# Row norms of a two-layer encoder at the stage handovers: root and reciprocal by token instead of spread over 128 rows

## The reference, cut to what matters

```python
def rms_norm(x, g=None):
    y = x * lax.rsqrt(jnp.mean(jnp.square(x), axis=-1, keepdims=True) + EPS)
    return y if g is None else y * g
def modulated_pre(x, g, mods, j):
    return rms_norm(x, g) * (1.0 + mods[:, 3 * j + 1, None]) + mods[:, 3 * j, None]
def gated_post(x, o, g, mods, j, coef):
    return x + coef * mods[:, 3 * j + 2, None] * rms_norm(o, g)
def layer(x, c, l, mixer):
    h = modulated_pre(x, norm_pre[l, 0], mods, 0)
    x = gated_post(x, swiglu(h, ...), norm_post[l, 0], mods, 0, 0.5)
    h = modulated_pre(x, norm_pre[l, 1], mods, 1)
    o, st = mixer(h, l)
    x = gated_post(x, o, norm_post[l, 1], mods, 1, 1.0)
    h = modulated_pre(x, norm_pre[l, 2], mods, 2)
    x = gated_post(x, swiglu(h, ...), norm_post[l, 2], mods, 2, 0.5)
```

## Time and profile before

| | us |
|---|---|
| median of 3 runs | 2572.78 |
| lowest, highest | 2572.46, 2575.69 |
| the profiled execution | 2575.32 |
| its span, first to last instruction | 2573.5 |

### The profile page before, as it was taken

How to read it: one execution, slowest core, us unless ns; L and a number is a source line. 1 busy time by engine, 2 the same in 40 slices (tenths; PEclk the granted TensorE clock), 3 DMA queues, 4 the chain that set the end, 5 groups by cost and what they waited for, 6 DMA issues and landing times.

```text
span 2573.5 us, 43848 instructions
## 1 busy us (share of the span) xinstructions
PE 2374.8 (92%) x17486; PEld 2231.6 (87%) x17486; DVE 1318.2 (51%) x2006; ACT 812.6 (32%) x1371; POOL 893.4 (35%) x384
## 2 busy tenths in 40 slices
PE   1999999899788899999989999989988898999996
PEld 1999999899456899999989999989964588999996
DVE  7333379784473333337253335986835515333552
ACT  2322322433223433223243223234323334223321
POOL 1333334443000544344444343444420034333342
PEclk9999999999899999999999999999989999999998
DMA  6222268323100122226312224761220011222551
GB/s 222 76 88 84 90 236 280 116 88 112 33 1 6 61 89 83 89 89 248 122 57 82 90 81 155 281 221 66 82 71 33 1 50 59 89 84 87 182 197 57
DMA packets 71507, 272.48 MB, mean 106 GB/s; under 512 B 8640, under 2 KB 10048, under 8 KB 70528
## 3 DMA queue, kind: packets, MB, share of 16 engines
q1 hardware_dynamic: 71424, 271.35, 30.6%
HBM read 267.87 MB, written 3.45 MB: 105 GB/s over the span
## 4 chain that ended last, share of the span: by engine, by line
PE 75%; DVE 12%; issue 6%; ACT 3%; DMA 1%; POOL 1%; DVEq 0%; SPq 0%; POOLq 0%; ACTq 0%
PE ps L534 21%; PE ps L533 21%; PE ps L537 21%; PE ps L543 2%; PE ps L831 2%; PE ps L875 2%; DVE ret_q L1407 1%; PE ps L827 1%; DVE ret_k L1407 1%; DVE wide_v L1297 1%; DVE x L1301 1%; PE ps L566 1%; DVE wide_v L1256 1%; POOL w_lo L446 1%; DVE ps L1290 1%
## 5 line engine op out<-in xcount | busy, mean ns | idle before, releaser
L446 POOL TENSOR_TENSOR w_lo<-raw,w_hi 128x1024 fp32r<-128x1024 f32 (+1 forms) x304 | 790.7, 2601 | 1609.8 <-ACT w_hi L947 1294.1
L533 PE MATMUL ps<-h_hi,w_hi 128*128 128x274 f32 x3296 | 897.0, 290 | 5.3 <-DVE z_tmp L1376 5.3
L534 PE MATMUL ps<-h_lo,w_hi 128*128 128x274 f32 x3296 | 900.7, 290 | 0.0
L537 PE MATMUL ps<-h_hi,w_lo 128*128 128x274 f32 x3296 | 686.7, 289 | 0.0
L533 PEld LDWEIGHTS ps<-h_hi,w_hi 128*128 128x128 f32 x3296 | 624.9, 190 | 6.8 <-issue 6.7
L534 PEld LDWEIGHTS ps<-h_lo,w_hi 128*128 128x128 f32 x3296 | 621.7, 189 | 0.2
L947 ACT CAST w_hi<-raw 128x1024 fp32r<-128x1024 f32 (+1 forms) x236 | 268.7, 1138 | 877.3 <-PE ps L537 689.8
L537 PEld LDWEIGHTS ps<-h_hi,w_lo 128*128 128x128 f32 x3296 | 522.0, 188 | 0.0
L533 PE MATMUL ps<-u_hi,w_hi 128*128 128x272 f32 x1408 | 382.4, 289 | 12.9 <-POOL w_lo L446 12.9
L534 PE MATMUL ps<-u_lo,w_hi 128*128 128x272 f32 x1408 | 380.8, 289 | 0.0
L1256 DVE CUSTOM_DVE_ANT_0 wide_v<-ada_w,ps 128x1024 bf16<-128x1024 f32 x288 | 332.1, 1217 | 46.5 <-DMA ada_w<-in_ada 29.3
(11 more groups left out here) (219 smaller groups left out, 2552.5 us busy)
## 6 DMA issues: line engine op xcount, KB each, us to landing
raw<-in_w_up SPq DMA_DIRECT2D x176, 512.0 KB, 3.3
ada_w<-in_ada SPq DMA_DIRECT2D x160, 512.0 KB, 4.4
raw<-in_w_dn SPq DMA_DIRECT2D x64, 704.0 KB, 4.7
raw<-in_w_mix SPq DMA_DIRECT2D x64, 512.0 KB, 3.3
decay<-in_decay SPq DMA_DIRECT2D x2, 2048.0 KB, 8.3
x<-in_x SPq DMA_DIRECT2D x1, 2176.0 KB, 9.1
rope_tab<-in_rope SPq DMA_DIRECT2D x2, 1088.0 KB, 4.9
out_y<-x SPq DMA_DIRECT2D x1, 2176.0 KB, 7.3
```

Of the source, the lines that this page charges most:

```text
L446: pool.tensor_tensor(w_lo[:, slot, 0:width], raw[:, slot, 0:width], w_hi[:, slot, 0:width].bitcast(F32), ALU.subtract).then_inc(lo_done.se ...
L533: pe.matmul(ps[:, bank + t, 0:half], wh, hi[:, n], start=start, stop=False)
L534: pe.matmul(ps[:, bank + t, 0:half], wh, lo[:, n], start=False, stop=False)
L537: last = pe.matmul(ps[:, bank + t, 0:half], wl, hi[:, n], start=False, stop=stop)
```

## The change

Each norm's sums are turned round. `token_sums` takes the tile of squares as the stationary operand, 128 tokens at a time, and a single column of ones as the moving one: five weight blocks (the last overlaps the fourth: tokens 416 to 543) and five matmuls of one column in place of two of 272. The sums land with tokens on partitions, 128x5, in unused columns of the second bank (`by_token`). ACT roots and DVE inverts those 128x5. Then `spread` brings them back: PE waits for the reciprocal and transposes each of the five columns, broadcast to 128 (32 in the last), so that all 128 partitions hold the 544 factors in the two banks. After a sub-layer DVE multiplies straight from there. Before one, DVE waits for the transposes and copies them to `rinv`; PE's wait on the root becomes a wait on that copy (`rinv_in`). `spread` stands at the end of `out_tiles` and at the end of `first_tiles`. The mixer's inner norms still use `add_squares` and `root_of`.

```diff
+TOK_AT = [0, P, 2 * P, 3 * P, T - P]
+TOK = len(TOK_AT)
+SUM_AT = 2 * NS
...
+        tok_root = sb("tok_root", [P, TOK])
+        tok_inv = sb("tok_inv", [P, TOK])
...
-        out_inv = pair(4)
+        def by_token(bank):
+            return ps[:, bank + 1, SUM_AT:SUM_AT + TOK]
+        def along(bank):
+            return ps[:, bank:bank + 2, :].rearrange("p b n -> p (b n)")[:, 0:T]
...
+            def token_sums(src, bank, start, stop):
+                for b, at in enumerate(TOK_AT):
+                    last = pe.matmul(by_token(bank)[:, b:b + 1], src[:, at:at + P], ones[:, 0:1],
+                                     start=start and b == 0, stop=stop, skip_group_check=True)
+                return last
+            def spread(l, n, bank):
+                pe.wait_ge(inverted.sem, inverted.at(l, n + 1))
+                for b in range(4):
+                    pe.transpose(ps[:, bank, b * P:(b + 1) * P], tok_inv[:, b:b + 1].to_broadcast([P, P]), ident[:, :])
+                pe.transpose(ps[:, bank + 1, 0:NS], tok_inv[P - NS:P, 4:5].to_broadcast([NS, P]),
+                             ident[P - NS:P, P - NS:P]).then_inc(inv_spread.sem, 1)
...
@@ first_tiles, pre_sum, early_sum
                 last.then_inc(w_used.sem, 1)
+                spread(l, 2 * j, 6)
...
-                add_squares(tmp_s[:, m % 2, :], 6, m == N_EARLY, False, ones).then_inc(sums.sem, 1)
+                token_sums(tmp_s[:, m % 2, :], 6, m == N_EARLY, False).then_inc(sums.sem, 1)
...
-                add_squares(squares[:, :], 6, False, True, ones).then_inc(sums.sem, 1)
+                token_sums(squares[:, :], 6, False, True).then_inc(sums.sem, 1)
...
@@ up (in the mixer likewise, rinv_in.at(l, 2))
-                pe.wait_ge(rooted.sem, rooted.at(l, 4 * s + 1))
+                pe.wait_ge(rinv_in.sem, rinv_in.at(l, 2 * s + 1))
...
@@ out_tiles
-                add_squares(squares[:, :], 4, True, False, ones)
+                token_sums(squares[:, :], 4, True, False)
                 pe.wait_ge(out_sq.sem, out_sq.at(l, (j + 1) * KD))
-                add_squares(tmp_s[:, 1, :], 4, False, True, ones).then_inc(sums.sem, 1)
+                token_sums(tmp_s[:, 1, :], 4, False, True).then_inc(sums.sem, 1)
+                spread(l, 2 * j + 1, 4)
...
@@ ACT, in pre_scale (bank 6) and out_tiles (bank 4)
+            def token_root(l, n, bank):
+                nc.scalar.activation(tok_root[:, :], by_token(bank), ACT.Sqrt, bias=eps[:, 0:1], scale=1.0 / D)\
+                    .then_inc(rooted.sem, 1)
...
@@ DVE turn_over, post
-                    v_.reciprocal(out_inv, halves(root[:, :])).then_inc(inverted.sem, 1)
-                    dve.wait_ge(inverted.sem, inverted.at(l, 2 * j + 2))
+                    v_.reciprocal(tok_inv[:, :], tok_root[:, :]).then_inc(inverted.sem, 1)
                     dve.wait_ge(out_ev.sem, out_ev.at(l, (j + 1) * KD))
+                    dve.wait_ge(inv_spread.sem, inv_spread.at(l, 2 * j + 2))
...
-                        v_.tensor_tensor(halves(tmp_v[:, m % 2, :]), halves(o_buf[:, m, :]), out_inv, ALU.mult)\
+                        v_.tensor_tensor(tmp_v[:, m % 2, :], o_buf[:, m, :], along(4), ALU.mult)\
...
@@ DVE turn_over, pre
-                    v_.reciprocal(rinv[:, :], root[:, :]).then_inc(inverted.sem, 1)
+                    v_.reciprocal(tok_inv[:, :], tok_root[:, :]).then_inc(inverted.sem, 1)
+                    dve.wait_ge(inv_spread.sem, inv_spread.at(l, 2 * j + 1))
+                    v_.tensor_copy(rinv[:, :], along(6)).then_inc(rinv_in.sem, 1)
```

More of the change, by code:

```diff
@@ L249, in streaming_trunk @@
         inverted = signal("inverted", 6)
+        inv_spread = signal("inv_spread", 6)
+        rinv_in = signal("rinv_in", 3)
         h_high = signal("h_high", 54)
@@ L663, in mixer @@
                 z_tile(3, 2, 1)
-                pe.wait_ge(rooted.sem, rooted.at(l, 3))
+                pe.wait_ge(rinv_in.sem, rinv_in.at(l, 2))
                 norm_sum(0, 0, 6, True, False)
@@ L985, in pre_scale @@
                 act.wait_ge(sums.sem, sums.at(l, (j + 1) * SUMS - 1))
-                root_of(l, rooted, 2 * j, 6, D)
+                token_root(l, 2 * j, 6)
                 high(l, next_chunk + 3, 1, KD * P)
@@ L1040, in out_tiles @@
                 act.wait_ge(sums.sem, sums.at(l, (j + 1) * SUMS))
-                root_of(l, rooted, 2 * j + 1, 4, D)
+                token_root(l, 2 * j + 1, 4)
             def ffn(l, s):
@@ L1325, in ffn @@
                         n = s * FT + i * 2 + f
-                        dve.wait_ge(inverted.sem, inverted.at(l, 4 * s + 1))
+                        dve.wait_ge(rinv_in.sem, rinv_in.at(l, 2 * s + 1))
                         dve.wait_ge(up_mul.sem, up_mul.at(l, 2 * n - 2))
@@ L1371, in z_scaled @@
                     dve.wait_ge(w_used.sem, w_used.at(l, MIX_C0 + z + 1))
-                    dve.wait_ge(inverted.sem, inverted.at(l, 3))
+                    dve.wait_ge(rinv_in.sem, rinv_in.at(l, 2))
                     if z >= 2:
```

## The result

| | before | after |
|---|---|---|
| median, us | 2572.6 (4 runs) | 2608.1 (4 runs) |
| lowest, highest | 2571.0, 2575.7 | 2607.0, 2610.2 |
| span of the profiled execution | 2573.5 | 2608.4 |

The changed kernel is slower: ratio 1.0128, 95% interval 1.0113 to 1.0142, or 36 us. The forecast was 2614.0 in a range of 2570 to 2631.

A forecast was written before the change was run, and what follows sets the result against it. PE was three quarters of the chain of waits, so time is won where PE idles. The profiled 2575.3 with -8.8 post, +7.5 pre and +43 clock gives 2616.8, for the median 2614; range 2570 to 2631.

The forecast's parts named there:

- The clock: Pre stages: PE falls to 1.2 GHz after two sums; 7.1 us a stage, 43 in six (24 to 60); chance 0.72.
- the doubled sums: Pre stage at half clock: three token sums take double the time, +3.35 us a stage.
- The rest of the spell in the next tile: After a pre stage: the half-clock stretch runs on into the next weight tile, +1.0 us a stage.
- the clock that holds: Rival: PE's clock doesn't fall in the pre stages; -1.3 us, 2571.5, no change; chance 0.16.
- Post: After a sub-layer: shorter chain from sum to first product; 1.2 us in five handovers, 2.75 in the last, 8.8 together.
- The wait for POOL: After a sub-layer: DVE's add to `x` ends 0.59 us after POOL's `w_lo`, so five handovers gain 1.2, not 2.75.
- Pre: Before a sub-layer, clock aside: removed root and reciprocal worth nothing, added weight loads and transposes cost 7.5 us in all.
- The row with the same load: Profile row for token sums: 128-column loads every 0.1115 us, so a sum of ten records takes 1.12 us.
- the row of narrow matmuls at 0.034: Profile row with 64-column weights and 32 moving columns, 0.034 us apart; lower bound of 0.34 us for a token sum.
- Cheap loads: Rival: weight loads of the token sums clearly under 0.09 us and the clock holds; 19.4 us faster, 2553; chance 0.06.
- spread stalls: Rival: PE's `spread` waits because ACT casts the next chunk before the root; some 2580 us; chance 0.03.
- chain not shortened: Rival: after a sub-layer the chain from sum to first product stays as long; takes off the 8.8, 2623; chance 0.03.

The follow-up runs named there:

- 128 columns: Changed kernel with the five pre sums moving 128 equal columns of ones per matmul in place of one: 2578.9 us, ratio 1.0011 to the kernel before.
- pre alone: Changed kernel with by-token norms only before a sub-layer, those after one as in the kernel before: 2616.4 us, ratio 1.0158 to the kernel before.
- runs with 32 columns: Changed kernel with the five pre sums moving 32 equal columns of ones per matmul in place of one: 2581.9 us, ratio 1.0024 to the kernel before.
- 64 and 128 columns: The 64-column version: changed kernel with pre sums moving 64 equal columns of ones per matmul in place of one: 2577.4 us, ratio 1.0008 to the kernel before.
- post alone: Changed kernel with by-token norms only after a sub-layer, those before one as in the kernel before: 2568.7 us, ratio 0.9978 to the kernel before.
- The cast moved ahead: By-token norms only after a sub-layer, with ACT's next-chunk cast and root before its last output copies: 2564.0 us, ratio 0.9955 to the kernel before.

## Why the prediction was right

**The clock, which decided.** It fell in all six pre stages, as forecast, and six stages cost 29.2 us by it in their own length (changed kernel against 128 columns). I had 3.35 + 2.0 + 0.75 = 6.1 a stage, 36.6 in all; measured are 4.2 to 6.3. The mis-sized term is the doubled sums: I let the clock fall after two sums everywhere. In the profile of the changed kernel it did so only before the mixers, the second and fifth sub-layers (stages of 17.2 and 16.7); in the other four it fell after three, so two were doubled and not three, 1.0 us less. That is no rule of these places: in pre alone, with the same pre stages, lengths are 14.0 to 16.7 and the clock fell before or within the third sum in four of six. What sets the place stays open. The second tile's 16 matmuls cost 1.7 more (4.00 against 2.28 with 128 columns; I had 2.0), `spread` 0.4 to 0.5 (0.75). The rest of the spell in the next tile was at most 0.5, not 1.0: after the first stage the third tile's first six matmuls take 1.37 us, with 128 columns 0.87. It was 0.4 to 0.5 in four stages, 0.1 in the fourth and nothing in the second, 1.9 in all where I had 6.
The evidence was weaker than I took it for. I argued from matmuls of 32 columns beside which the clock stayed at 1.2 GHz. The runs with 32 columns show that this width, once the clock is at 2.4 GHz, holds it in five stages of six. What the row showed was a clock that was down already and didn't rise, in a stretch where PE also had gaps; that it would fall under single columns didn't follow from it, and the 0.16 for the clock that holds was low for what was known. That the clock fell in all six stages was therefore partly luck.
The Trainium skill, page "TensorE: Matmul & The Clock Gate", section Part 1: The HAM clock gate, ties the clock to the array's activity. The runs agree in so far as less was computed in the stages that fell (six, one, none and none of six with 1, 32, 64 and 128 columns); the profile's busy columns are not a measure of it, since they are full on both sides.

**Post.** Forecast 8.8, measured 8.6. The chain by its terms, from post alone: the sum ends 0.23 later (forecast 0.24), root 0.27 (0.22), reciprocal 0.19 (0.18), transposes 0.82 (0.8), and from them to the product 0.11 (0.04). The first product starts 3.80 us after the first sum's start, 2.64 earlier than before; I had 2.75. That a 128x5 root and reciprocal could be had from 128x1 and 128x544 by a line was right to 0.05 us. The wait for POOL was right: 0.59 after POOL's end was the assumption, 0.57 and 0.58 were measured, and 1.19 of 1.2 us were gained. The cast moved ahead gives the other 1.45 back in the stage, which only a run could show.

**Pre.** The token sums: ten loads every 0.1118 us, 1.17 by the records, forecast 0.1115; at half clock 0.213. The row with the same load was the right one, and the row of narrow matmuls at 0.034 was not. The growth without the clock came to 1.72 + 5 x 1.09 = 7.2 against the 7.5 of the sum, `spread` 0.69 of the 0.75. Root, reciprocal and copy hid as said: DVE still waits 4.5 us for PE before its copy at 81.1.
The Trainium skill's section LDWEIGHTS on the page just named, columns / 1.2, gives 107 ns for these loads, as an estimate. The 0.112 measured agrees within 5% at 2.4 GHz; at 1.2 GHz a load takes 0.213, about twice that, so the rule holds for one of the clock's levels.

**What was missing.** The stretches between: +6.5 us, for which the forecast had nothing but the 1.0 a stage of the clock's rest. 2.8 are the tiles' address, by reckoning, and 1.9 the rest of the spells. About 0.6 more are the third tile's start, which I had at nothing: its first six matmuls take 0.87 us behind the transposes even at full clock, 0.77 in the kernel before. The last 1.2 lie within what single stretches vary by, as does the start (64.8 to 66.5 us among all profiles). Together: -8.6 + 7.2 + 29.2 + 6.5 + 0.7 (start) = 35.0, where I had -8.8 + 7.5 + 43 = 41.7 (the recorded sum says 41.5, a slip of 0.2). Of the clock's 43 came 29.2 + 1.9, so I had 12 too many, and 5.3 us that I had not foreseen (4.6 between, 0.7 at the start) took part of that back. The forecast of 2614.0 is thus nearer to 2608.1 than its terms are to theirs, which is luck too.

**The rivals.** "The clock holds" was built by the runs with 64 and 128 columns: 2577.4 and 2578.9 where I had 1.3 less than before. Its step, gain 8.8 against loss 7.5, was right; the stretches between made it slower, the address a part of them. So even with the clock held the pre part earns nothing: it takes 7.2 us to hide what was hidden. "Cheap loads" fell with the 0.1118; "spread stalls" and "chain not shortened" didn't occur.

## What to carry to other kernels

Take a reduction that is spread over all partitions to a few columns only where the chain it shortens is exposed: here after the sub-layer (ratio 0.9955 with POOL's work out of the way), not before it, where a weight tile covered it already. When narrow matmuls take the place of wide ones, ask what the array still computes: a sum of single columns behind full weight loads kept PE busy by the records of these profiles and let its clock fall; here 64 equal columns in place of one cost nothing and kept it up. And compare the rate of an untouched matmul loop before blaming the change for the rest: here two small tiles declared ahead of the large ones slowed one kind of loop more than they sped up the other, and behind them they changed neither rate.

## What the runs showed of the hardware that I had not expected

- 40 bytes of shift of the operands in SBUF change the rate of a full matmul loop: 127.36 to 127.9 ns at 274 columns, the same in every profile of a kernel with the one or the other layout, and 125.7 to 125.3 at 272 (without the shift, one down loop of four came to 126.0 or 126.1).
- PE's records and those of its weight loads are gapless (3.40 of 3.40 us) both where the clock is 1.00 and where it is 0.50. Only the granted clock tells, or the length of a record (a load of 128 columns: 0.112 or 0.213 us).
- The fp32 sum with 128x128 weights takes ten loads whatever it moves: 1.17, 1.20, 1.22 and 1.28 us by the records at 1, 32, 64 and 128 columns.
- With the loads between them, 32 columns a matmul held 2.4 GHz in five stages of the one profile taken and lost it in a sixth, at the same order of the same instructions. So two places of one execution can differ in it; why stays open.
